# Requesting half of each batch's cache pages from ScalarE's queue in a two-layer hybrid decoder step

## The chip, the cores and the metric

One core of one Trainium2 chip runs the whole program. The metric is the time of one execution in device microseconds (us), median of three runs. Engines are named as in the profile: PE is TensorE, PEld its weight load, DVE VectorE, ACT ScalarE, POOL GpSimd, SP SyncE, which computes nothing and asks for transfers. A q behind a name (SPq, ACTq) is the sequencer of that engine: register work, semaphore waits, DMA issues.

## What is computed

Two decoder layers, for 256 prompt tokens and 8 batches of 8 sample tokens that share all weights. A layer is four parallel token mixers between an input and an output projection, then a feed-forward block. The part that the change touches is the attention of the sample tokens on a paged cache: each of the 8 batches reads its own 8 pages of 128 rows by a page table.

```python
def mla_sample_attention(q_abs, q_pe, ckv, kpe, past):
    ...
    s_past = (jnp.einsum('bqhr,bkr->bhqk', q_abs, pc) + jnp.einsum('bqhp,bkp->bhqk', q_pe, pp)) * scale
    s_new = (jnp.einsum('bqhr,bkr->bhqk', q_abs, ckv) + jnp.einsum('bqhp,bkp->bhqk', q_pe, kpe)) * scale
    ...
    p = jax.nn.softmax(jnp.concatenate([s_past, s_new], axis=-1).astype(jnp.float32), axis=-1)
    return jnp.einsum('bhqk,bkr->bqhr', p[..., :P], pc) + jnp.einsum('bhqk,bkr->bqhr', p[..., P:], ckv)
```

## The kernel before, in words

**Order.** A hardware loop runs the layer body twice. Each engine has a program of its own, written out by hand, and engines meet at semaphores: `ev` counts an event up, `at` gives the value to wait for. Weights stand in HBM as blocks of 128 x 2048 float32 (1 MB) in the order of use, and go through a ring of three buffers, `ring`. SP walks through the blocks in one loop: `load_block(n)` (L950) waits until PE is done with block n-3 and asks for block n. Where the walk reaches certain blocks, SP does other transfers too.

**Splitting.** An input projection block is used in three parts. ACT copies each half of it to a rounded form `wh` (`high`, L1063, two copies of 1024 columns), POOL subtracts it from the block to get the rest, `wlx` (L2015), and PE multiplies with both (L429, L430, then L434). So PE can't start a projection tile before ACT's copy of its half.

**The stretch of the sample batches** is a loop over b = 0 to 7 on each engine. On PE (L820 to L833) iteration b does `sample_back(b-2)`, `sample_turn(b-1)`, `sample_scores(b)` (L736: queries against the 8 pages of batch b, after a wait for all 8), `sample_values(b-1)` (L760), and then a slot of other work that keeps PE busy: gate tiles (the split kind), `branch` blocks (L413) or adaLN blocks, `ada` (L463, with transposes at L453). On ACT (L1323 to L1333) iteration b copies out results of the earlier batches (`sample_back`, `sample_turned`), does the softmax exponentials of batch b (`sample_exp`: one of 128x512 and one of 64x64), in iteration 3 also the squares for the convolution's norm (`conv_squares`), and then what its slot needs: `high` for a coming gate block, sigmoids of gates, copies of ada rows to `rowb`. All of ACT's rows have line 1046, that of the helper `go`.

```python
SLOTS = [[("gate", 2, 0)],
         [("ada", 8), ("gate", 2, 2), ("ada", 9)],
         [("ada", 10), ("ada", 11), ("ada", 12)],
         [("ada", 13), ("ada", 14), ("ada", 15)],
         [("branch", 2, 0), ("gate", 2, 4), ("ada", 16)],
```

**Pages.** The cache has two buffers of 8 pages, one for even and one for odd batches, in `arena`. `load_pages(b)` (L963) runs on SP. It reads the 8 page numbers from SBUF into registers (`value_load`, L965: a TENSOR_LOAD and two register instructions each), waits until PE has done `sample_values(b-2)`, the last reader of that buffer (semaphore pe_m, label so), and issues 8 DMAs (L973) of 128 rows x 2560 B, 320 KB each. For b from 2 on it stands behind the load of block `SLOT_START[b - 1] + 2`, and the loads of the next blocks stand behind it.

Of the kernel before, what the change touches and what calls it, by code (L numbers as in the profile page):

```python
# [24 lines left out]
D_MODEL, SEQ, DEPTH, NB, TS, PAST, PAGE = 1024, 256, 2, 8, 8, 1024, 128  # L25
# [9 lines left out]
NPG = PAST // PAGE  # L35
POOL = NB * NPG * 5 // 4
# [148 lines left out]
class Counts:  # L185
# [21 lines left out]
    def at(self, name, label):  # L207

        return self.sem(name), self.known[name, label] if self.known else 1


def decoder_program(nc, a, known):

    ctx = ExitStack()
    with ctx:
        place = {}

        def sb(name, shape, dt=F32):
            place[name] = (nc.sbuf_base + 31) // 32 * 32
            return ctx.enter_context(nc.sbuf_tensor(name, shape, dt))  # L220
# [5 lines left out]
        C = Counts(nc, ctx, known)  # L226
        ev, at = C.ev, C.at
# [41 lines left out]
        pages = sb("pages", [1, NB * NPG], I32)  # L269
# [5 lines left out]
        def part(n, shape, names, rows=P, start=None):  # L275
            o = used[0] if start is None else start
            v = arena[:, o:o + n].rearrange(f"p ({names}) -> p {names}", **shape) if shape else arena[:, o:o + n]
            if start is None:
                used[0] += n
            assert o + n <= ARENA  # L280
            return v
# [26 lines left out]
        cache = part(2 * NPG * 640, dict(r=2, g=NPG, f=640), "r g f")  # L308
# [73 lines left out]
        with nc.Fori(0, DEPTH) as layer:  # L382
            with nc.Block() as block:
# [556 lines left out]
                def _(sp):  # L940
# [21 lines left out]

                    def load_pages(b):  # L963
                        r = b % 2
                        pgs = [sp.value_load(pages[0:1, b * NPG + g:b * NPG + g + 1], min_val=0, max_val=POOL - 1) for g in range(NPG)]  # L965
                        if b >= 2:
                            sp.wait_ge(*at("pe_m", ("so", b - 2)))
                        else:

                            sp.wait_ge(*at("dve_dc", (NB - 1, 3)))  # L970
                            sp.wait_ge(C.sem("out_state_dp" if b == 0 else "out_state_d"), 16)
                        for g, pg in enumerate(pgs):
                            sp.dma_start(cache[:, r, g, :], a["cache"][lay, bass.ds(pg, 1), :, :].rearrange("l n p f -> (l n p) f")  # L973
                                         ).then_inc(C.sem(f"in_cache{r}"), 16)

                    first_gate = BLOCKS.index(("in", "g0_0", "g0_1"))
                    for n in range(NBLK):
# [37 lines left out]
                        if n == SLOT_START[0]:  # L1015
                            load_pages(0)
# [4 lines left out]
                        if n == SLOT_START[0] + 1:  # L1021
                            load_pages(1)

                        for b in range(2, NB):
                            if n == SLOT_START[b - 1] + RING - 1:
                                load_pages(b)
# [14 lines left out]
                def _(act):  # L1041
                    act.wait_ge(C.sem("in_small"), 16)

                    def go(sem, label, out, in_, func, **kw):
                        in_turn(act, "act")
                        return nc.scalar.activation(out, in_, func, **kw).then_inc(*ev(sem, label))  # L1046
# [5 lines left out]
                    def m(name):  # L1052
                        act.wait_ge(*at("pe_m", name))
                        return banks[name]

                    def ada(a0, a1):
                        for i in range(a0, a1):
                            ps = z(("ada", i))
                            if i >= 2:
                                act.wait_ge(*at("pe_m", ("adaT", i // 2 - 1)))  # L1060
                            go("act_mod", i, rowb[:, i % 2, :], ps[:, 0:256], ACT.Copy)
# [218 lines left out]
                    def conv_squares():  # L1280
                        act.wait_ge(C.sem("out_conv"), 32)
                        for j in range(4):
                            act.wait_ge(*at("dve_c", ("mu", j)))
                            go("act_cy", ("sq", j), sqc[:, j, :], y[:, 2, j, :], ACT.Square)

                    def conv_silu():
                        go("act_cy", "std", std[:], m("conv var")[:, 0:T], ACT.Sqrt, bias=cs("eps")[:, 0:1], scale=1.0 / CCH)
                        for j in range(4):
                            act.wait_ge(*at("dve_c", ("xn", j)))
                            go("act_cy", j, y[:, 2, j, :], y[:, 2, j, :], ACT.Silu, bias=sw("clb", j), scale=sw("clg", j))  # L1290

                    def sample_exp(b):
                        r = b % 2
                        act.wait_ge(*at("dve_s2", ("nm", b)))
                        if b >= 2:
                            act.wait_ge(*at("pe_m", ("sT", b - 2)))
                        go("act_s", ("e", b, 0), pb[:, r, 0:512], m(("ss", b))[:, :], ACT.Exp, bias=stats[:, 100 + r:101 + r], scale=BSCALE,
                           accum_out=stats[:, 104 + 2 * r:105 + 2 * r])
                        go("act_s", ("e", b, 1), pb[0:NS, r, 512:576], pb[0:NS, r, 512:576], ACT.Exp,
                           bias=stats[0:NS, 100 + r:101 + r], scale=BSCALE, accum_out=stats[0:NS, 105 + 2 * r:106 + 2 * r])  # L1300

                    def sample_turned(b):
                        if b >= 2:
                            act.wait_ge(*at("pe_m", ("so", b - 2)))
                        go("act_s", ("pT", b), pT[:, b % 2, 0:512], m(("sT", b))[:, :], ACT.Copy)

                    def sample_back(b):
                        ps = m(("soT", b))
                        go("act_s", ("oT", b), olatT[:, :, :, b * TS:(b + 1) * TS], ps[:, 0:2 * NS].rearrange("p (c h t) -> p c h t", c=2, h=BH), ACT.Copy)

                    def slot(b):
                        for kind, *which in SLOTS[b]:
                            if kind == "gate":
                                gates(*which, count=2, follow=which[0] == 1)
                            elif kind == "branch" and which == [2, 0]:
                                high(SPLIT.index(("in", "g2_4", "g2_5")))
                            elif kind == "ada":
                                nxt = BLOCKS[BLOCKS.index((kind, which[0])) + 1]
                                if nxt in SPLIT and which[0] < 18:
                                    high(SPLIT.index(nxt))  # L1320
                                ada(which[0], which[0] + 1)

                    for b in range(NB):  # L1323
                        if b >= 2:
                            sample_back(b - 2)
                        if b >= 1:
                            sample_turned(b - 1)
                        sample_exp(b)
                        if b == CONV_NORM:
                            conv_squares()  # L1330
                        slot(b)
                        if b == CONV_NORM:
                            conv_silu()  # L1333
# [915 lines left out]
```

## Time and profile before

| | |
|---|---|
| median of 3 runs | 1873.16 us (1868.24 to 1875.08) |
| the profiled execution | 1869.28 us |
| its span, first to last instruction | 1867.3 us |
| PE busy | 1706.9 us, 91% of the span |
| DVE, ACT, POOL busy | 43%, 39%, 38% |
| mean granted PE clock | 0.96 of full |
| DMA | 309 MB, mean 166 GB/s |
| stretch of the sample batches | about 431 to 600 us, and 1359 to 1528 us |

Times of rows are in us from the span's start. Busy rows of a timeline merge neighbouring instructions of one kind; the bracket behind a row gives the idle time of the engine before it and what ended it. The two layers repeat each other closely, so the first stands for both where nothing else is said.

### The profile page before, as it was taken

What the parts mean: (1) busy time and instruction counts of PE and PEld (TensorE: products, weight loads), DVE (VectorE), ACT (ScalarE), POOL (GpSimd) and SP (SyncE); (2) the same over time, 40 slices, a digit from 0 to 9 for tenths busy, and PEclk for the clock granted to TensorE, in tenths of its full rate; (3) what the DMA queues carried; (4) which work ended last, traced back from release to release, by engine and by line L of the source; (5) the groups of instructions that cost most, each with busy time, mean ns of one, the idle gap of its engine ahead of it and who ended that gap; (6) DMA issues with size and microseconds to landing.
All of it is one profiled execution on the core that took longest, in us unless ns stands there. A gap on an engine that the chain in (4) does not pass through costs nothing.

```text
span 1867.3 us, 30317 instructions
## 1 busy us (share of the span) xinstructions
PE 1706.9 (91%) x10994; PEld 1470.4 (79%) x10994; DVE 806.9 (43%) x1887; ACT 735.0 (39%) x1110; POOL 700.8 (38%) x438
## 2 busy tenths in 40 slices
PE   3899999999799989999838999999997999899997
PEld 1788899886477869999717888998864778799996
DVE  0445386655331353332314544876553223533233
ACT  1455534334333244442314564442333432444332
POOL 0434555544122423333113445564531234233331
PEclk9899999999899989999968999999998999899999
DMA  9243335248765344443072523362587643434440
GB/s 352 97 177 114 102 108 204 91 164 305 282 228 201 118 181 149 145 159 135 29 287 91 188 92 102 111 215 85 176 313 281 240 171 127 183 141 157 148 145 29
DMA packets 73246, 309.10 MB, mean 166 GB/s; under 512 B 15554, under 2 KB 25090, under 8 KB 43010
## 3 DMA queue, kind: packets, MB, share of 16 engines
q1 hardware_dynamic: 73090, 307.09, 45.8%
q8 instruction: 90, 1.47, 0.3%
q14 instruction: 66, 0.54, 0.1%
HBM read 291.81 MB, written 15.25 MB: 164 GB/s over the span
## 4 chain that ended last, share of the span: by engine, by line
PE 39%; DVE 6%; DMA 2%; issue 1%; ACT 1%; SPq 1%; DVEq 0%; ACTq 0%
PE zps L429 5%; PE zps L434 5%; PE zps L430 4%; PE zps L890 4%; PE zps L891 4%; PE zps L892 4%; PE zps L413 4%; DMA ring<-wpack_dram 1%; PE mps L736 1%; PE mps L413 1%; DVE arena L1689 1%; PE mps L760 1%; DMA arena<-cache_dram 1%; PE zps L463 1%; PE mps L641 1%
## 5 line engine op out<-in xcount | busy, mean ns | idle before, releaser
L2015 POOL TENSOR_TENSOR wlx<-ring,wh 128x1024 fp32r<-128x1024 f32 x172 | 409.3, 2379 | 708.1 <-ACT wh L1046 702.2
L429 PE MATMUL zps<-uhi,wh 128*128 128x320 f32 x1232 | 380.4, 321 | 1.8 <-ACT wh L1046 1.7
L430 PE MATMUL zps<-ulo,wh 128*128 128x320 f32 x1232 | 367.7, 311 | 0.0
L1046 ACT ACTIVATE wh<-ring 128x1024 fp32r<-128x1024 f32 x172 | 182.3, 1060 | 356.2 <-PE zps L430 252.7
L2115 POOL TENSOR_TENSOR wlo<-ring,whi 128x1024 fp32r<-128x1024 f32 x66 | 160.2, 2427 | 311.2 <-ACT whi L1046 310.3
L429 PEld LDWEIGHTS zps<-uhi,wh 128*128 128x128 f32 x1232 | 235.0, 191 | 14.4 <-issue 9.2
L430 PEld LDWEIGHTS zps<-ulo,wh 128*128 128x128 f32 x1232 | 235.0, 191 | 0.8
L890 PE MATMUL zps<-xhi,whi 128*128 128x320 f32 x688 | 213.8, 311 | 0.0
L891 PE MATMUL zps<-xlo,whi 128*128 128x320 f32 x688 | 213.3, 310 | 0.0
L892 PE MATMUL zps<-xhi,wlo 128*128 128x320 f32 x688 | 213.2, 310 | 0.0
L434 PE MATMUL zps<-uhi,wlx 128*128 128x320 f32 x1248 | 210.5, 311 | 0.0
L434 PEld LDWEIGHTS zps<-uhi,wlx 128*128 128x128 f32 x1248 | 191.1, 190 | 0.1
L1046 ACT ACTIVATE whi<-ring 128x1024 fp32r<-128x1024 f32 x132 | 140.1, 1061 | 102.0 <-PE zps L892 93.9
L413 PE MATMUL zps<-y,ring 128*128 128x320 f32 x512 | 143.9, 438 | 1.0 <-issue 1.0
L1046 ACT ACT_TABLE_LOAD x74 | 94.9, 1283 | 113.0 <-PE mps L736 43.2
L890 PEld LDWEIGHTS zps<-xhi,whi 128*128 128x128 f32 x688 | 130.0, 189 | 0.0
L891 PEld LDWEIGHTS zps<-xlo,whi 128*128 128x128 f32 x688 | 130.0, 189 | 0.0
L892 PEld LDWEIGHTS zps<-xhi,wlo 128*128 128x128 f32 x688 | 129.8, 189 | 0.0
L413 PEld LDWEIGHTS zps<-y,ring 128*128 128x128 f32 x512 | 96.6, 192 | 42.0 <-issue 4.1
L1956 DVE TENSOR_TENSOR wlo<-ring,whi 128x1024 fp32r<-128x1024 f32 x64 | 78.4, 1226 | 102.0 <-ACT whi L1046 101.6
L890 PE MATMUL zps<-hhi,whi 128*128 128x320 f32 x352 | 111.3, 316 | 3.4 <-DVE hlo L1990 3.4
L463 PE MATMUL zps<-ring,siluc 128*32 128x256 f32 x768 | 59.5, 438 | 58.9 <-DMA ring<-wpack_dram 58.9
(279 smaller groups left out, 2548.6 us busy)
## 6 DMA issues: line engine op xcount, KB each, us to landing
ring<-wpack_dram SPq DMA_DIRECT2D x222, 1024.0 KB, 4.9
arena<-cache_dram SPq DMA_DIRECT2D x128, 320.0 KB, 4.9
arena<-stateA_dram SPq DMA_DIRECT2D x2, 2064.0 KB, 9.7
o_cn_s<-arena SPq DMA_DIRECT2D x2, 2064.0 KB, 11.2
arena<-stateD_dram SPq DMA_DIRECT2D x2, 2048.0 KB, 11.9
o_ret_s<-arena SPq DMA_DIRECT2D x2, 2048.0 KB, 11.6
x<-o_y SPq DMA_DIRECT2D x2, 1280.0 KB, 10.1
o_y<-x SPq DMA_DIRECT2D x4, 640.0 KB, 3.0
```

The costliest lines, as they stand in the source:

```text
L413: last = nc.tensor.matmul(o, l, r, start=i == 0, stop=i == len(mms) - 1)
L429: nc.tensor.matmul(o, hi[:, k * P:(k + 1) * P], xh[:, k, :], start=k == 0, stop=False)
L430: last = nc.tensor.matmul(o, hi[:, k * P:(k + 1) * P], xl[:, k, :], start=False, stop=False)
L434: last = nc.tensor.matmul(o, wlx[:, n % RING, (j * KC + k) * P:(j * KC + k + 1) * P], xh[:, k, :], start=False, stop=k == KC - 1)
L463: last = nc.tensor.matmul(ps[g:g + 32, 0:256], siluc[:, k, :], w[:, k * 256:(k + 1) * 256], start=k < 4, stop=k >= 4)
L890: nc.tensor.matmul(o, hi[:, cols], xh, start=start, stop=False)
L891: nc.tensor.matmul(o, hi[:, cols], xl, start=False, stop=False)
L892: return nc.tensor.matmul(o, lo[:, cols], xh, start=False, stop=stop)
L1046: return nc.scalar.activation(out, in_, func, **kw).then_inc(*ev(sem, label))
L1956: V().tensor_tensor(wlo[q % 2][:, 0:1024], ring[:, FFN_AT[q] % RING, 0:1024], whi[q % 2][:, 0:1024], ALU.subtract).then_inc(*ev("dve_w", q))
L2015: G().tensor_tensor(wlx[:, n % RING, half], ring[:, n % RING, half], wh[:, i, :], ALU.subtract).then_inc(*ev("pool_l", (q, i)))
L2115: G().tensor_tensor(wlo[q % 2][:, 1024:2048], ring[:, FFN_AT[q] % RING, 1024:2048], whi[q % 2][:, 1024:2048], ALU.subtract).then_inc(*ev(" ...
```

## The change

SP asks for all 8 pages of batches 0 and 1 as before, but only for pages 0 to 3 of batches 2 to 7. ACT gets a `load_pages` of its own, with its own register loads and its own wait, and asks for pages 4 to 7 of batch b+1 in iteration b (1 to 6), between `sample_exp(b)` and the rest of the iteration. PE's wait for 8 pages is as before.

```diff
                     def load_pages(b):
                         r = b % 2
-                        pgs = [sp.value_load(pages[0:1, b * NPG + g:b * NPG + g + 1], min_val=0, max_val=POOL - 1) for g in range(NPG)]
+                        mine = range(NPG) if b < 2 else range(NPG // 2)
+                        pgs = [sp.value_load(pages[0:1, b * NPG + g:b * NPG + g + 1], min_val=0, max_val=POOL - 1) for g in mine]
...
+                    def load_pages(b):
+
+                        r, half = b % 2, range(NPG // 2, NPG)
+                        pgs = [act.value_load(pages[0:1, b * NPG + g:b * NPG + g + 1], min_val=0, max_val=POOL - 1) for g in half]
+                        act.wait_ge(*at("pe_m", ("so", b - 2)))
+                        for g, pg in zip(half, pgs):
+                            act.dma_start(cache[:, r, g, :], a["cache"][bass.ds(layer, 1), bass.ds(pg, 1), :, :].rearrange("l n p f -> (l n p) f")
+                                          ).then_inc(C.sem(f"in_cache{r}"), 16)
+
                     for b in range(NB):
                         if b >= 2:
                             sample_back(b - 2)
                         if b >= 1:
                             sample_turned(b - 1)
                         sample_exp(b)
+                        if 1 <= b < NB - 1:
+                            load_pages(b + 1)
                         if b == CONV_NORM:
                             conv_squares()
                         slot(b)
```

On ACT, in iteration 1, this stood between the second exponential and the split of gate block g2_2 before:

```order
L1046 ACT_TABLE_LOAD [waits act_s,pe_m]
L1046 ACTIVATE arena,stats<-mps,stats 128x512 [waits dve_s2]
L1046 ACTIVATE arena,stats<-arena,stats 64x64 [waits act_s]
L1046 ACTIVATE wh<-ring 128x1024 [waits pool_l,act_s,pe_h,w_landed0]
L1046 ACTIVATE wh<-ring 128x1024 [waits act_hq,pool_l,pe_h]
L1046 ACTIVATE rowb<-zps 128x256 [waits act_hq,pe_m,pe_z]
```

and this stands there now (line 1047 is 1046 of before; TENSOR_LOAD with two ISA rows is there four times, ISA with DMA four times):

```order
L1047 ACTIVATE arena,stats<-arena,stats 64x64 [waits act_s]
L1327 TENSOR_LOAD pages
L1327 ISA x2
...
L1330 ISA [waits pe_m]
L1330 DMA arena<-cache_dram 128x640
...
L1047 ACTIVATE wh<-ring 128x1024 [waits pool_l,act_s,pe_h,w_landed0]
```

The split copies now come behind four register loads, a wait for PE and four DMA issues of the same queue. The other five iterations, 2 to 6, get the same piece.

## Rows read from the trace of the kernel before

**Rows 1.** The page, part 1: busy us, share of the span, instructions.

```profile
PE 1706.9 (91%) x10994; PEld 1470.4 (79%) x10994; DVE 806.9 (43%) x1887; ACT 735.0 (39%) x1110; POOL 700.8 (38%) x438
```

**Rows 2.** Waits, 400 to 600 us, then 1330 to 1530 us: total, times, longest.

```profile
PE mps L736 <- DMA arena<-cache_dram: 6.7, 3, 5.8
...
PE mps L736 <- DMA arena<-cache_dram: 6.4, 2, 6.2
```

**Rows 3.** Timeline of PE, iterations 1 to 4: start, us, instruction, idle before and releaser.

```profile
450.39 0.39 PE L429 MATMUL zps<-uhi,wh 128*128 128x320 f32 x1 [0.86 <-ACT wh L1046]
...
476.79 3.68 PE L736 MATMUL mps<-arena,qabs 128*64 128x512 f32 x8 [5.84 <-DMA arena<-cache_dram]
...
490.56 0.66 PE L453 MATMUL mps<-const,rowb 128*128 128x128 f32 x4 [1.46 <-ACT rowb L1046]
...
501.27 0.45 PE L413 MATMUL mps<-ckv,qabs 128*64 128x64 f32 x4 [2.21 <-ACT arena L1046]
```

**Rows 4.** Timeline of SP's DMA issues for batches 2 and 3, and blocks behind.

```profile
448.80 4.74 SPq L973 DMA_DIRECT2D arena<-cache_dram  x8
...
466.15 4.80 SPq L973 DMA_DIRECT2D arena<-cache_dram  x8
471.13 1.93 SPq L961 DMA_DIRECT2D ring<-wpack_dram  x3
```

**Rows 5.** Line 965, 442 to 448 us: duration ns, first and last start.

```profile
L965 SPq TENSOR_LOAD <-pages x8: 263/266/272, 442.5 to 446.4; - x8
```

**Rows 6.** Timeline of ACT, iteration 1.

```profile
445.81 1.28 ACT L1046 ACT_TABLE_LOAD   x1 [2.54 <-PE mps L736]
...
448.64 0.35 ACT L1046 ACTIVATE arena<-arena,stats 64x64 f32<-64x64 f32 x1
...
449.19 2.23 ACT L1046 ACTIVATE wh<-ring 128x1024 fp32r<-128x1024 f32 x2
```

**Rows 7.** Line 1070, 448 to 449 us, first sequencer instruction after that exponential.

```profile
L1070 ACTq EVENT_SEMAPHORE  x1: 17/17/17, 448.6 to 448.6; - x1
```

**Rows 8.** Stretches: us, PE, PEld, DVE, ACT, POOL busy, PEclk, DMA share, GB/s.

```profile
466.00:468.00 2.00, 2.00 (x32) 1.09 (x28) 1.23 (x5) 0.83 (x4) 0.00 (x0) 1.00 0.44 119
468.00:470.00 2.00, 2.00 (x35) 1.25 (x24) 0.09 (x2) 0.38 (x1) 0.00 (x0) 1.00 0.85 256
470.00:472.00 2.00, 0.95 (x8) 0.64 (x7) 1.97 (x6) 1.26 (x3) 0.00 (x0) 1.00 0.85 300
472.00:474.00 2.00, 0.00 (x0) 0.00 (x0) 1.08 (x4) 0.00 (x0) 0.00 (x0) 1.00 0.94 321
474.00:476.00 2.00, 0.00 (x0) 0.00 (x0) 0.00 (x0) 0.00 (x0) 0.00 (x0) 0.58 1.05 417
...
480.00:482.00 2.00, 2.00 (x10) 0.55 (x8) 0.04 (x1) 0.00 (x0) 0.00 (x0) 0.72 1.01 422
...
677.00:679.00 2.00, 2.00 (x9) 2.00 (x9) 1.73 (x3) 1.92 (x2) 0.97 (x1) 0.50 0.00 0
```

**Rows 9.** Timeline of PE, first matmul of the feed-forward block.

```profile
672.91 1.41 PE L898 MATMUL zps<-xhi,whi 128*128 128x320 f32 x4 [3.74 <-ACT xhi L1046]
```

**Rows 10.** Timeline of ACT, iteration 3: second exponential, squares.

```profile
485.03 0.35 ACT L1046 ACTIVATE arena<-arena,stats 64x64 f32<-64x64 f32 x1
...
487.86 2.16 ACT L1046 ACTIVATE acc<-y 128x320 f32<-128x320 f32 x4 [2.38 <-DVE y L1834]
```

**Rows 11.** Timeline of ACT, iterations 4, 5 and 6: first work after the exponentials.

```profile
505.12 2.23 ACT L1046 ACTIVATE wh<-ring 128x1024 fp32r<-128x1024 f32 x2
...
535.80 1.28 ACT L1046 ACT_TABLE_LOAD   x1 [3.22 <-PE zps L434]
...
558.64 1.06 ACT L1046 ACTIVATE wh<-ring 128x1024 fp32r<-128x1024 f32 x1 [2.06 <-PE zps L430]
```

**Rows 12.** Timeline of PE: where those gate tiles are used.

```profile
516.02 0.55 PE L429 MATMUL zps<-uhi,wh 128*128 128x320 f32 x1
...
565.43 1.34 PE L434 MATMUL zps<-uhi,wlx 128*128 128x320 f32 x8
```

## The prediction

> **What bounds the kernel now.** I read the page first: PE is busy for 91% of the span [rows 1], so time can be won only in PE's gaps and is lost wherever PE is made to wait. In the waits of the sample stretch the pages cost PE 6.7 us in the first layer and 6.4 us in the second, nearly all of it in one wait per layer [rows 2]: PE sits 5.84 us at the scores of batch 3 [rows 3]. That is what the change could win. The timeline of SP shows the reason: the eight requests for batch 3 go out from 466.15 us, when the buffer has just come free, and take 4.80 us to issue; three ring blocks follow at 471.13 [rows 4]. The timelines of PE and ACT then show what the change could cost: PE already waits for ACT's `wh` copy in iteration 1 (0.86 us), for a `rowb` copy in iteration 3 (1.46 us) and for a copy at the scores of batch 4 (2.21 us) [rows 3]. ACT is on the path exactly there, though it is busy only 39% of the span [rows 1].
>
> **What a batch costs ACT.** Four register loads: on SP eight of them start from 442.5 to 446.4 us, 0.56 us apart [rows 5], so four take 2.2 us. Four issues: SP's eight take 4.74 us [rows 4], 0.59 each, so four take 2.4 us. No row shows ACT doing either; from below I bound the sum at 3.5 us (4 x 0.27 us, the loads without what follows them, and 2.4 us), from above at 6 us (a third more for each instruction), and take SP's 4.6 us, the same instructions on another sequencer. Where do they start? In program order they follow the second exponential. The first sequencer instruction behind it now, a wait for something long done, is at 448.6 us [rows 7], when that exponential starts (448.64) and not when the table load before it went out (445.81) [rows 6]. So ACT's sequencer gets free about at the start of the second exponential, and I count from there.
>
> **Iteration 1 (pages of batch 2).** 448.64 + 4.6 = 453.2 us: the `wh` copies start then instead of at 449.19 [rows 6], 4.05 us later. The wait for PE's values of batch 0 costs nothing, since SP passes the same wait at 448.8 [rows 4]. PE waits for this copy already [rows 3], so nothing covers it: **+4.05 us**, and PE stands still for 4.9 us. After the gap of 3.74 us at 672.91 [rows 9] the granted clock was 0.50 of full, the 1.2 GHz level, still at 677 to 679 [rows 8]; in the 5.84 us gap it fell to a mean of 0.58 in 474 to 476 us, and came back during 480 to 482 (0.72, so low for 1.1 us of it) [rows 8]. There it cost half of the 4.3 us from 476.8 to 481.1, 2.2 us. For iteration 1 I take **+2.5 us**, between nothing (the clock holds) and 3.1 us (half of the 6.1 us from 672.9 to 679).
>
> **Iteration 2 (pages of batch 3).** ACT's copies of ada rows come up to 4 us later, and PE's transposes with them; the cover is PE's wait for pages until 476.79 [rows 3]. The question is when the last page lands. SP's half is out by 468.6 us, as before. ACT's half starts at 466.1 + 2.2 = 468.3 and is out by 470.7, no sooner than pages 4 to 7 were. The pages are not limited by the issuing alone: while they move, the DMA engines are 85 to 94% busy at 256 to 321 GB/s [rows 8]. Had they been the limit of nothing, 2.3 us of issuing saved would come back whole; as it is, the best case is 1 us sooner. New is that SP's three ring blocks (3 MB) are now asked for at 468.7, 2.4 us sooner, on one queue, beside ACT's pages on another. By 469.5 us SP's half has moved about 0.6 MB of its 1.31 MB (2 us at 119 and 1.5 us at 256 GB/s [rows 8]). At equal shares of 300 GB/s its rest ends near 474.1, ACT's half having moved 0.7 MB too; the last 0.6 MB of ACT's run beside the ring blocks. If both queues get equal bytes of 420 GB/s [rows 8], they land at 477.1, 0.3 us later than now; if they take turns row by row, 2560 B against 8192 B, ACT's get a quarter, 100 GB/s, and land at 480.3, 3.5 us later. I take the middle, **+2.0 us**, with -1 and +3.5 as ends. The Trainium skill ("DMA: Bandwidth & Descriptors", section on queues, rings and completion order) says that an engine takes turns between queues packet by packet; by that rule alone the sum would stand at the upper end, and no row of before shows two data queues at once. The same page (issuing engines are not separate DMA queues) holds that issuing from several engines saves only issue time; the busy shares of 85 to 94% agree.
>
> **Iteration 3 (pages of batch 4).** From 485.03, ACT is held until 489.65; the squares start at 487.86 now [rows 10], so they come 1.8 us later. Behind them is the `rowb` copy for which PE waits at 490.56 [rows 3], then the variance, the convolution's norm and the copy for which PE waits at 501.27: **+1.8 us**. This also covers pages of batch 4 that land up to about 4 us late.
>
> **Iterations 4 to 6: nothing.** In 4 the copies at 505.12 [rows 11] slide by 4 us as in iteration 1, to about 509.3, and are used from 516.02 [rows 12]; PE's branch block is the cover. In 5 the table load at 535.80 came after 3.22 us of idle time, so the second exponential started 3.66 us ahead of it, and it slides by 0.9 us. In 6 the copy at 558.64 [rows 11], with 2.06 us of idle time ahead, slides by 2.1 us; its half is multiplied from about 563 and its rest at 565.43 [rows 12], after POOL's 2.4 us, which leaves some 1 us. If PE's cover were gone each would cost what it slides. SP's shorter issue brings ring blocks sooner, but PE waits for none of them there.
>
> **Sum.** 4.05 + 2.5 + 2.0 + 1.8 = 10.35 us per layer, 20.7 us for two. The profiled execution took 1869.3 us, so 1890.0; it lay 3.9 us under the median, so against the median of 1873.2 I forecast **1893.9 us**, 1.1% slower. From the ends: least 2 x (2.95 + 0 - 1 + 0.7) = 5.3 us, if ACT's loads and issues take 3.5 us; most 2 x (5.45 + 3.1 + 3.5 + 3.2) = 30.5 us.
>
> **Rivals.**
> - *ACT's sequencer runs ahead.* The Trainium skill ("Perfetto Trace Analysis", section on DVE and ACT instructions) says that a sequencer is free once it has pushed an instruction into a wait queue. As a mechanism of this kernel: the loads run in the time in which ACT waits for DVE's maximum, from 445.8 on, and only the issues (2.4 us from 448.6) are left. Iteration 1 then costs 451.0 - 449.2 = 1.8 us, iteration 3 nothing (its issues end at 487.5, before the squares), and batch 3's pages, all asked for by 468.5, land 1 us sooner: 2 x 0.8 = 1.6 us, 1875. For it: ACT idles 2.54 us ahead of that table load [rows 6]. Against it: rows 7. Chance 0.12.
> - *The clock holds and the pages aren't late.* Only ACT's stalls are left: 2 x 5.85 = 11.7 us, 1885. For it: PE had stood still for 3 us by 474, at a clock still at 1.00 [rows 8]. Part of the forecast's family; 0.2.
> - *The pages of batch 3 come early enough, the other side.* If two queues moved them 3.8 us sooner (landing by 473), PE's gap there would be 2 us, the 2.2 us of low clock would go too, and with the run-ahead of the first rival the layer would win 3.8 + 2.2 - 1.8 = 4.2 us: 1865. It decides only where the landing comes forward by more than ACT's own delay on the path, 1.8 us at the least and 5.85 us by my count. Against it: the 2.6 MB of a batch need 6.2 us even at 420 GB/s, from 467.4 at the earliest, so 473.6 at best. Chance 0.04.
> - *The change doesn't do what it says.* The order of instructions shows 4 of 8 requests on ACT for six batches; only batches 0 and 1 are left out. Chance nil.
>
> **How the numbers follow.** Forecast as summed 0.64, only the stalls 0.2, run-ahead 0.12, faster 0.04. About 0.5% (9.4 us) is what a measurement of this kernel can tell from no change. The two first cases are over it but for their lower edge, 0.06 of them: slower 0.78; same 0.06 + 0.12 + part of the last = 0.19; faster 0.03. The range runs from 1881 (stalls at the short end) to 1904 (all costs at their upper ends); it leaves out the run-ahead, the faster case and the tails.
>
> **What would show it.** Right: 48 of 128 page requests on ACT's sequencer, some 4.6 us from the first register load to the last issue; PE's wait on `wh` at the first split tile of iteration 1 near 5 us with a stretch of clock 0.50 behind it; PE's wait on `rowb` in iteration 3 over 3 us; the wait for pages of batch 3 no shorter than before. Wrong: register loads on ACT ahead of the exponentials, a page wait well under 4 us, or an unchanged wait in iteration 1.

## The result and the profile after

The changed kernel takes 1905.73 us (median of 4 runs, 1903.99 to 1906.86); the kernel before, with one more run beside it, 1870.76 us. The ratio is 1.0189, with a 95% interval of 1.0169 to 1.0209. Forecast were 1893.9 us and a range of 1881 to 1904: the sign was right, the size was not. The sum gave 20.7 us; about 35 us were lost.

The change does what it says. From the DMA table of the changed kernel (engine, count, KB each, median us from issue to landing):

```profile
arena<-cache_dram SPq DMA_DIRECT2D x80, 320.0 KB, 4.3
arena<-cache_dram ACTq DMA_DIRECT2D x48, 320.0 KB, 7.2
```

48 of 128 page requests are ACT's, and they land later after their issue than SP's do. PE's timeline in the first layer, against [rows 3]:

```profile
455.13 0.60 PE L429 MATMUL zps<-uhi,wh 128*128 128x320 f32 x1 [5.27 <-ACT wh L1047]
...
479.04 0.66 PE L453 MATMUL mps<-const,rowb 128*128 128x128 f32 x4 [2.52 <-ACT rowb L1047]
...
490.68 3.68 PE L736 MATMUL mps<-arena,qabs 128*64 128x512 f32 x8 [9.97 <-DMA arena<-cache_dram]
...
506.80 1.12 PE L453 MATMUL mps<-const,rowb 128*128 128x128 f32 x4 [3.91 <-ACT rowb L1047]
...
515.69 1.94 PE L736 MATMUL mps<-arena,qabs 128*64 128x512 f32 x8 [1.50 <-DMA arena<-cache_dram]
```

The wait for `wh` grew from 0.86 to 5.27 us, that for pages of batch 3 from 5.84 to 9.97, with 2.52 us for `rowb` ahead of it, and in iteration 3 there are 3.91 us for `rowb` and 1.50 for pages of batch 4. In the second layer the same waits are 5.29, 10.38, 3.66 and, for batch 4:

```profile
1461.73 3.68 PE L736 MATMUL mps<-arena,qabs 128*64 128x512 f32 x8 [4.33 <-DMA arena<-cache_dram]
```

The times between the first score matmuls (L736) of consecutive batches, from the timelines of both kernels, show where the 37.6 us between the two profiled spans (1867.3 and 1904.9) lie. The rest of the program adds 0.4 us.

| us, first layer / second | before | after |
|---|---|---|
| batch 1 to 2 (iteration 1) | 17.4 / 17.4 | 24.2 / 24.3 |
| batch 2 to 3 | 16.9 / 17.4 | 23.6 / 24.3 |
| batch 3 to 4 | 19.3 / 18.5 | 25.0 / 25.0 |
| batch 4 to 5 | 29.9 / 30.4 | 27.5 / 30.4 |
| batches 5 to 7 | 45.2 / 45.2 | 45.2 / 45.2 |

ACT's timeline in iteration 1 and SP's and ACT's issues for batch 3, against [rows 4, 6]:

```profile
448.96 0.35 ACT L1047 ACTIVATE arena<-arena,stats 64x64 f32<-64x64 f32 x1
449.22 0.19 ACT L1047 ACTIVATION_READ_ACCUMULATOR arena<-arena,stats 64x1 f32 x1
451.57 2.18 ACTq L1330 DMA_DIRECT2D arena<-cache_dram  x4
453.93 2.23 ACT L1047 ACTIVATE wh<-ring 128x1024 fp32r<-128x1024 f32 x2 [4.53 <-issue]
...
475.56 2.42 ACTq L1330 DMA_DIRECT2D arena<-cache_dram  x4
```

```profile
473.31 2.06 SPq L974 DMA_DIRECT2D arena<-cache_dram  x4
475.57 1.53 SPq L961 DMA_DIRECT2D ring<-wpack_dram  x3
```

ACT's queue needs 4.97 us from the second exponential to the copies (forecast 4.6). For batch 3, ACT's first request goes out in the same hundredth of a microsecond as SP's first ring block. The stretches around it (columns as in [rows 8]):

```profile
474.00:476.00 2.00, 2.00 (x36) 1.32 (x36) 0.66 (x3) 0.00 (x0) 0.00 (x0) 1.00 0.79 265
476.00:478.00 2.00, 0.52 (x12) 0.04 (x4) 0.00 (x0) 0.00 (x0) 0.00 (x0) 1.00 0.95 291
478.00:480.00 2.00, 0.96 (x9) 0.96 (x10) 0.27 (x1) 0.99 (x3) 0.00 (x0) 1.00 1.07 396
...
486.00:488.00 2.00, 0.00 (x0) 0.00 (x0) 0.00 (x0) 0.00 (x0) 0.00 (x0) 0.50 1.01 423
488.00:490.00 2.00, 0.00 (x0) 0.00 (x0) 0.00 (x0) 0.00 (x0) 0.00 (x0) 0.50 0.68 271
```

By 478 us the engines have moved 1.1 MB, all of it from SP's half of the pages (1.3 MB). In the DMA records of this trace (one for each row moved) ACT's first row starts at 478.12 us and the first ring row at 478.06. All of ACT's half then goes beside 3 MB of ring blocks, at 396 to 423 GB/s in total, and both end together near 490.

### The profile page after: what moved, and what is told of

Its sections match the earlier page's. It is cut to its first block and busy times, and to the rows that moved or that the text cites. A ratio compares the mean times of both kernels' runs of the same rounds, so it can differ in the third digit from the quotient of the medians.

```text
span 1904.9 us, 30321 instructions
## 1 busy us (share of the span) xinstructions
PE 1713.8 (90%) x10994; PEld 1476.3 (78%) x10994; DVE 799.8 (42%) x1887; ACT 735.0 (39%) x1110; POOL 700.5 (37%) x438
## 5 line engine op out<-in xcount | busy, mean ns | idle before, releaser
L429 PE MATMUL zps<-uhi,wh 128*128 128x320 f32 x1232 | 383.5, 323 | 10.7 <-ACT wh L1047 10.6
L1047 ACT ACTIVATE whi<-ring 128x1024 fp32r<-128x1024 f32 x132 | 140.1, 1061 | 101.4 <-PE zps L892 93.9
## 6 DMA issues: line engine op xcount, KB each, us to landing
o_cn_s<-arena SPq DMA_DIRECT2D x2, 2064.0 KB, 11.4
arena<-stateD_dram SPq DMA_DIRECT2D x2, 2048.0 KB, 11.9
```

The lines of the kernel that those rows point to most:

```text
L429: nc.tensor.matmul(o, hi[:, k * P:(k + 1) * P], xh[:, k, :], start=k == 0, stop=False)
```

## The experiments

**1. Nothing on ACT in iteration 1.**

```diff
-mine = range(NPG) if b < 2 else range(NPG // 2)      # SP
+mine = range(NPG) if b < 3 else range(NPG // 2)
-if 1 <= b < NB - 1: load_pages(b + 1)                # ACT
+if 2 <= b < NB - 1: load_pages(b + 1)
```

> Edit: SP asks for all eight pages of batch 2; ACT asks for its half only for batches 3 to 7, so iteration 1 has no page work on ACT. Theory (ACT's stall in front of the wh copies, with the low clock behind it, is a term of its own): PE's wait at the first split tile of iteration 1 falls from 5.3 us back to 0.9, no clock of 0.5 follows at 454 us, the scores of batch 2 start near 460 us as before the change; 2 x (4.4 + 2.4) = 13.6 us come back, about 1892 us. The wait for pages of batch 3 stays at 10 us. Rival (all of the loss is that pages land late): iteration 1 costs nothing net, the time stays within 3 us of 1905.7.

Measured: 1891.87 us, ratio to before 1.0115 (1.0082 to 1.0149). PE's timeline:

```profile
450.27 0.38 PE L429 MATMUL zps<-uhi,wh 128*128 128x320 f32 x1 [0.85 <-ACT wh L1047]
...
483.93 3.68 PE L736 MATMUL mps<-arena,qabs 128*64 128x512 f32 x8 [10.34 <-DMA arena<-cache_dram]
```

Batch 1 to 2 takes 17.4 us again in both layers, so ACT's stall and the low clock behind it cost 6.8 and 6.9 us there, and 13.9 us of the median went, as forecast. The pages of batch 3 stay as late: a term of its own.

**2. Ring blocks held back until the pages have landed.**

```diff
 if n == SLOT_START[b - 1] + RING - 1:
     load_pages(b)
+    sp.wait_ge(C.sem(f"in_cache{b % 2}"), 16 * NPG * (b // 2 + 1))
```

> Edit: the changed kernel, but SP waits until all eight pages of a batch (2 to 7) have landed before it asks for the next ring blocks, so no ring row shares the DMA engines with ACT's pages. Theory (ring blocks on SP's queue take three quarters of the bandwidth from ACT's pages): pages of batch 3 land 7 us or less after ACT's last request, PE's wait for them falls from 10 us to between 4 and 7 us, the extra wait for pages of batch 4 goes; 4 to 8 us come back, about 1899 us, less what PE then waits for late ring blocks. Rival (ACT's pages are late because ACT asks late, or because its queue is slow): the landing from ACT's queue stays near 12 us in iteration 2 and the time rises, as ring blocks come later too.

Measured: 1889.65 us, ratio 1.0106 (1.0068 to 1.0144), more than forecast. Line 1331, ACT's requests for batch 3, and PE's timeline:

```profile
DMA to landing us min/median/max: 4.9/5.2/5.8
```

```profile
488.23 3.68 PE L736 MATMUL mps<-arena,qabs 128*64 128x512 f32 x8 [2.47 <-DMA arena<-cache_dram]
```

In the changed kernel the same requests took this long:

```profile
DMA to landing us min/median/max: 7.9/11.7/13.3
```

With no ring block beside it ACT's queue is about as quick as SP's was before the change (median 5.2 us against 4.9), and PE's page wait falls to 2.5 us, with 2.13 us for `rowb` ahead of it. So the ring blocks were what made the pages late. Batch 2 to 3 takes 16.0 us in both layers, 0.9 and 1.4 us less than before the change: PE starts the scores of batch 3 9.7 us after SP's first request, where the kernel before needed 10.6 and 11.1, although ACT still asks 2.2 us after SP. That is a small gain of two queues. Late ring blocks cost PE nothing that its waits show in the stretch. In the first layer batch 0 to 1 took 16.0 us instead of 11.4, at a clock of 0.50 from 434 to 444 us; but SP asks for batch 2 only at 455.43 us, and the edit first acts behind that, so this isn't its doing.

**3. The register loads alone, in the kernel before.**

```diff
 sample_exp(b)
+if 1 <= b < NB - 1:
+    for g in range(NPG // 2, NPG):
+        act.value_load(pages[0:1, (b + 1) * NPG + g:(b + 1) * NPG + g + 1], min_val=0, max_val=POOL - 1)
```

> Edit: the kernel before, with ACT's four register loads in iterations 1 to 6 and nothing else of the change. It prices the loads: 4 x 0.56 = 2.2 us behind the second exponential. Theory (ACT's sequencer doesn't run ahead): the wh copies of iteration 1 start 1.8 to 2.2 us later, PE waits 2.7 to 3.1 us there; iteration 3 costs nothing (487.3 is before 487.86); 2 x 2 = 4 us slower, up to 8 if the clock falls after a gap of 3 us: 1875 to 1879. Rival (the sequencer runs ahead and the loads are free): same as before within 1 us.

Measured: 1875.44 us, ratio 1.0024 (1.0002 to 1.0046). PE waits 2.82 us for `wh` in the first layer, 2.60 in the second. ACT's timeline:

```profile
447.78 0.35 ACT L1046 ACTIVATE arena<-arena,stats 64x64 f32<-64x64 f32 x1
448.04 0.19 ACT L1046 ACTIVATION_READ_ACCUMULATOR arena<-arena,stats 64x1 f32 x1
450.30 2.23 ACT L1046 ACTIVATE wh<-ring 128x1024 fp32r<-128x1024 f32 x2 [2.08 <-issue]
```

2.08 us of ACT's idle time follow the exponential: the loads don't run ahead of it, and four of them cost about what SP's rows said (2.2 us). Scores of batch 0 to those of batch 7 take 142.7 and 142.3 us, against 140.1 and 140.2.

**4. The register loads ahead of the exponentials, in the changed kernel.**

```diff
+if 1 <= b < NB - 1:
+    pgs = page_numbers(b + 1)      # the four value_loads
 sample_exp(b)
 if 1 <= b < NB - 1:
-    load_pages(b + 1)
+    load_pages(b + 1, pgs)         # the wait and the four requests
```

> Edit: the changed kernel, with ACT's four register loads ahead of the exponentials, where ACT waits for DVE's maximum, and its wait and four requests where they were. Theory: the loads are covered in part (ACT idles 2.3 us ahead of the table load and 1.0 behind it), so the stall behind the exponentials shrinks from 4.5 to about 2.3 us: PE's wait in iteration 1 falls from 5.3 to about 3.1, that for rowb in iteration 3 by 2, and ACT asks 2.2 us sooner in iteration 2, so that ACT's pages get onto the engines ahead of the ring blocks and land 3 us sooner. 2 x 5 to 2 x 8 us come back: 1890 to 1896. Rival (the late pages don't depend on when ACT asks): 2 x 3 us come back, 1900.

Measured: 1877.42 us, ratio 1.0032 (1.0013 to 1.0052), far more than either expected: 28.3 of 35 us came back. The issues for batch 3, SP's and ACT's, and what PE waits:

```profile
468.39 2.05 SPq L974 DMA_DIRECT2D arena<-cache_dram  x4
470.62 1.50 SPq L961 DMA_DIRECT2D ring<-wpack_dram  x3
```

```profile
L1334 ACTq DMA_DIRECT2D arena<-cache_dram x4: 348/356/375, 468.5 to 470.2; - x4
...
DMA to landing us min/median/max: 3.8/5.9/9.0
```

```profile
479.27 3.42 PE L736 MATMUL mps<-arena,qabs 128*64 128x512 f32 x8 [5.99 <-DMA arena<-cache_dram]
```

With the loads out of the way ACT asks at 468.5 us beside SP's 468.39, its last request 0.4 us ahead of the first ring block, and the pages are there 10.9 us after SP's first request, where one queue alone needed 10.6 [rows 3, 4]. In the changed kernel it was 17.4 us, so 2.2 us in the time of asking decide over 6.5 us in the landing. The DMA records tell why: from 472 to 476 us the two queues moved 291 and 314 rows of pages, and the first ring row comes at 475.92, when about nine tenths of the page rows have started. In this order of requests two queues win nothing: the wait for batch 3 is 5.99 us, where it was 5.84. It is not the best that the change could do. ACT's last rows still run beside ring blocks here, and with the ring blocks held back (experiment 2) the pages came about 1 us sooner than from one queue. Both edits together were not run.

**5. and 6. Narrower ring rows.**

```diff
-sp.dma_start(ring[:, n % RING, :], src).then_inc(C.sem(f"w_landed{n % RING}"), 16)
+for h in range(2):
+    sp.dma_start(ring[:, n % RING, h * 1024:(h + 1) * 1024], src[:, h * 1024:(h + 1) * 1024]).then_inc(C.sem(f"w_landed{n % RING}"), 16)
```

(waits for `w_landed` count by 32 then)

> Edit: the changed kernel, each ring block asked for as two DMAs of 4096 B rows instead of one of 8192 B; nothing else. Theory (while both queues have work, the DMA engines take one row from each in turn): beside 4096 B rows ACT's 2560 B rows get 38% instead of 24% of the bandwidth, so the 512 rows of ACT's half pass at about 60 per us instead of 39 and pages of batch 3 land 3 to 4 us sooner; PE's wait falls from 10 us to 6 or 7 us and the one at batch 4 goes; 6 to 10 us come back over the two layers, about 1897 us, less what the doubled ring requests cost (see the control). Rival (equal bytes for each queue, or the later request alone): the wait stays at 10 us within 1 us.

> Edit: the kernel before with the same split ring blocks, as the control of the run above. Both theories: one queue alone, so no change in sharing; the second request costs SP 0.5 us a block, hidden behind PE. Within 3 us of before.

Measured: 1909.52 us, ratio 1.0190 (1.0148 to 1.0232); the control 1876.39, ratio 1.0030 (1.0003 to 1.0057). The waits for pages of batch 3 in the two layers:

```profile
491.50 3.68 PE L736 MATMUL mps<-arena,qabs 128*64 128x512 f32 x8 [6.67 <-DMA arena<-cache_dram]
...
1443.34 3.68 PE L736 MATMUL mps<-arena,qabs 128*64 128x512 f32 x8 [8.71 <-DMA arena<-cache_dram]
```

They fell by 3.3 and 1.7 us and the wait for batch 4 went. Part of the 3.3 us only moved to `rowb` (3.20 us instead of 2.52); from SP's first request to the scores it is 1.6 and 1.9 us less, where 3 to 4 were forecast. The time did not fall. From the scores of batch 0 to those of batch 7 the kernel takes 156.1 and 154.4 us (changed kernel 156.9 and 160.5), but outside of that the profiled execution loses 11.8 us. The control's loses 1.8 there, so the doubled requests alone don't explain it; why stays open. What settles how two queues share is the DMA records, rows started by each queue:

| | ring rows (SP's queue) | page rows (ACT's queue) |
|---|---|---|
| changed kernel, 480 to 488 us, ring rows of 8192 B | 310 | 304 |
| experiment 5, 484 to 489 us, ring rows of 4096 B | 304 | 300 |

In the second layer they are 307 and 324, and 302 and 301. The counts are near equal however wide the ring's rows are: turns by row, not by bytes. ACT's pages went from 38 to 60 rows per us, as the theory said, and with equal bytes they would have had some three rows for each ring row in the first case.

**7. Keys before values, one queue.** The scores read only a page's key part, the values only the rest, so the key part's space is free a good part of an iteration earlier. The edit is to the kernel before; PE then waits for each part where it reads it, and the host packs a page's keys ahead of its values.

```diff
-sp.wait_ge(*at("pe_m", ("so", b - 2)))
+sp.wait_ge(*at("pe_m", ("ss", b - 2)))
-    sp.dma_start(cache[:, r, g, :], a["cache"][lay, bass.ds(pg, 1), :, :]...).then_inc(C.sem(f"in_cache{r}"), 16)
+for part_, c0, c1 in (("keys", 0, 3 * P), ("values", 3 * P, 5 * P)):
+    if part_ == "values" and b >= 2:
+        sp.wait_ge(*at("pe_m", ("so", b - 2)))
+    for g, pg in enumerate(pgs):
+        sp.dma_start(cache[:, r, g, c0:c1], a["cache"][lay, bass.ds(pg, 1), :, c0:c1]...).then_inc(C.sem(f"in_{part_}{r}"), 16)
```

> Edit: the kernel before, all requests on SP, but a page comes as two DMAs: its key part (1536 B rows, read by the scores) is asked for when the scores of batch b-2 are done, its value part (1024 B rows, read by the values) when the values of batch b-2 are done; the host packs the page's columns as keys, rotary keys, values. Theory (the 5.8 us wait for pages of batch 3 is there because all of a page is asked for only when the last reader of its buffer is done): the key parts of batch 3 go out from about 464 us instead of 466.15 and in half the bytes, and land near 472 us, when PE gets there at 471; the wait falls to 0 to 2 us, the low clock behind it goes; 2 x 5 to 2 x 7.5 us: 1855 to 1860. Rival (the stretch is bound by what the DMA engines move, 5.8 MB between 466 and 484 us): PE waits for the ring blocks of ada 13 instead, and the time stays within 5 us of before.

Measured: 1868.67 us, ratio 0.9989 (0.9968 to 1.0009): no change, and neither theory as told. PE's timeline:

```profile
455.14 0.39 PE L429 MATMUL zps<-uhi,wh 128*128 128x320 f32 x1 [3.09 <-ACT wh L1050]
...
478.44 1.94 PE L736 MATMUL mps<-arena,qabs 128*64 128x512 f32 x8 [1.28 <-DMA arena<-cache_dram]
...
489.66 1.07 PE L463 MATMUL zps<-ring,siluc 128*32 128x256 f32 x16 [1.44 <-DMA ring<-wpack_dram]
```

The wait for batch 3 did fall to 1.3 us in the first layer, where the matmuls run at full clock (1.94 us instead of 3.68), and to 1.7 in the second, where they stay slow (3.50). It was lost again in iteration 1: SP's 16 requests for batch 1 take 8.9 us and stand ahead of the ring block of which `wh` is made.

**8. Experiments 1 and 4 together.** Both edits, in the changed kernel.

> Edit: the changed kernel with the register loads ahead of the exponentials and ACT's half only from batch 3 on, so nothing is left in front of the wh copies of iteration 1. Theory: PE's wait there falls from 2.8 to 0.9 us; 2 x 1.9 = 3.8 us less than 1877.4, about 1873; what is left of the change is a wash, since the wait for pages of batch 3 stays near 6 us (two queues move the pages no faster than one). Rival (two queues do help once ACT asks early): the wait for pages of batch 3 below 5 us and the time under 1868.

Measured: 1875.39 us (about 1873 expected), ratio 1.0009 (0.9982 to 1.0035), no difference from before that can be told. Page waits at batch 3 of 5.90 and 7.12 us: with the ring blocks right behind them, two queues move the pages no faster than one.

**9. Keys before values, whole pages for batches 0 and 1.** Against experiment 7:

```diff
-for part_, c0, c1 in (("keys", 0, 3 * P), ("values", 3 * P, 5 * P)):
+for part_, c0, c1 in (("keys", 0, 3 * P), ("values", 3 * P, 5 * P)) if b >= 2 else (("keys", 0, 5 * P),):
```

> Edit: the version with key parts before value parts, but batches 0 and 1, whose buffers are free at once, are asked for in whole pages again (8 requests instead of 16). Theory (what that version won at batch 3 it gave back in iteration 1, where 16 requests of SP's for batch 1 pushed the ring block of gate g2_2 back, and where 16 for batch 2 stand ahead of the next blocks): PE's wait for wh in iteration 1 falls from 3.1 and 2.0 us to 0.9, 2 x 2 to 2 x 3.5 us come back, 1862 to 1865. Rival (the loss of iteration 1 has another cause, such as the shorter rows): no change against that version, 1868.

Measured: **1858.47 us**, ratio 0.9947 (0.9929 to 0.9965), better than forecast (1862 to 1865). `wh` is on time again and the page wait stays short:

```profile
450.11 0.39 PE L429 MATMUL zps<-uhi,wh 128*128 128x320 f32 x1 [0.86 <-ACT wh L1051]
...
473.16 2.37 PE L736 MATMUL mps<-arena,qabs 128*64 128x512 f32 x8 [2.46 <-DMA arena<-cache_dram]
```

**10. The same, value parts one ring block later.**

```diff
+if n == SLOT_START[b - 1] + RING:
+    page_parts(b, "values", 3 * P, 5 * P)      # waits for ("so", b - 2), then 8 requests
 if n == SLOT_START[b - 1] + RING - 1:
-    load_pages(b)                              # both parts
+    load_pages(b)                              # key parts
```

> Edit: as the run above, and the value parts of batches 2 to 7 are asked for one ring block later, behind the first of the blocks that follow the key parts. Theory (SP's issue queue is what delays the ring blocks of the ada slots, and the value parts aren't needed for a whole iteration): PE's waits for ring blocks at the ada blocks of iteration 3 go too (1.4 and 0.9 us), batch 3's keys land as soon as before; 1857 to 1863. Rival (bytes bound the stretch, 5.8 MB in 18 us): the same bytes come in another order, and the time stays within 3 us of the run above.

Measured: 1858.92 us, ratio 0.9932 (0.9914 to 0.9950): the same as experiment 9 within noise, which the rival forecast; that bytes are the bound is not shown by it. The waits for ring blocks did not go: PE waits 1.12 and 0.68 us for them in the second layer. Both versions beat the kernel before and the changed one.

## Why the prediction was right and wrong

**ACT's price and place: right.** The loads don't run ahead (experiment 3), the whole piece holds the copies up by 4.4 us where 4.05 were forecast, and with the clock iteration 1 cost 6.8 and 6.9 us against 6.55; experiment 1 gave it back. The four signs named for being right all came, but they test the mechanism of the stall and not the size of the whole. The clock row of the changed kernel behind that wait:

```profile
456.00:458.00 2.00, 2.00 (x10) 2.00 (x9) 0.00 (x0) 0.55 (x2) 1.86 (x2) 0.50 0.98 391
```

**Iteration 2: the mis-sized term.** The forecast was +2.0 us with an upper end of 3.5; 6.7 and 6.9 us were measured. The step that failed is "its rest ends near 474.1, ACT's half having moved 0.7 MB too": I let ACT's bytes flow about one microsecond after its first request and share the engines with SP's pages. In fact 452 of SP's 512 rows had started before ACT's first, and ACT had moved 0.15 MB and not 0.7 when SP's half was through; for ACT asks 2.2 us later than SP and its first row comes 2.6 us behind that, so all 1.3 MB of ACT's went beside the ring blocks, not 0.6 MB. Of the two ways of sharing that I set as ends, turns by row was the right one, by the row counts under experiment 5: 1.31 MB at a quarter of 420 GB/s is 12.5 us, and ACT's rows took 11.9 us from the first to the last. The rule of the Trainium skill ("DMA: Bandwidth & Descriptors", section on queues, rings and completion order) is packet by packet in turn. The equal counts of rows agree with it if the packets of both queues hold as many rows, which no record here shows. The middle between the ends was no estimate but a refusal to choose; the upper end would still have been 3.2 and 3.4 us short, since it left only 0.6 MB for the ring blocks to hold up.

The time from SP's first request for batch 3 to PE's first score matmul puts the runs side by side:

| us, first layer / second | |
|---|---|
| kernel before: one queue | 10.6 / 11.1 |
| changed: ACT asks 2.2 us late | 17.4 / 18.0 |
| experiment 5: the same, ring rows of 4096 B | 15.8 / 16.1 |
| experiment 2: late, but ring blocks held back | 9.7 / 9.7 |
| experiment 4: ACT asks at once | 10.9 / 10.7 |

**Iteration 3: too low.** +1.8 us forecast, 5.7 and 6.5 measured. ACT's stall for `rowb` was +2.4 and +2.2 us, near the forecast. The rest is the sentence that the stall "also covers pages of batch 4 that land up to about 4 us late": they share the engines with ring blocks just as batch 3's do, and PE waited 1.5 and 4.3 us for them, where it had waited 0.5 and 0. In the second layer the two waits make up the whole 6.5 us. In the first they make 3.4 of 5.7; the matmuls from 506.80 to 513 us took 2.4 us more than before, at a clock of 0.50 to 0.53 up to 512, which is the rest. There 2.4 us came back between batches 4 and 5, where the kernel before had its own low stretch.

**Iterations 4 to 6: right**, 45.2 us in both kernels from batch 5 to 7, and no loss from batch 4 to 5. **The rivals.** Run-ahead fell with experiment 3. The faster case, which needed pages 3.8 us sooner, didn't come even when both queues asked at once (experiments 4 and 8), nor with the ring blocks held back, where the gain was about 1 us; the two together are untested. "DMA: Bandwidth & Descriptors" of the Trainium skill says in its section on issuing engines that a second engine saves only issue time, and the 10.9 against 10.6 us agree.

The terms don't add up quite: experiments 1 and 2 give back 14 and 16 us of 35 and experiment 4 alone 28, since an earlier request mends the stall in part and the lateness wholly. In experiment 4 nearly all of what is left lies in iteration 1, 3.4 and 3.5 us.

## What to carry to other kernels

In this kernel a second DMA queue added next to no bandwidth; it added a competitor. If one half of what somebody waits for goes to another queue and arrives there later than the first queue's next large transfers, it is served in turns with them, here row for row, so that narrow rows lose against wide ones, and the whole is as late as its last part. Put instructions on an engine that seems idle only after reading what stands behind them, register loads included, and place them where that engine waits anyway. And where a transfer waits for its buffer, ask first which part of the buffer the next reader needs: that, not the queue, was where the time lay here.

## What the runs showed of the hardware that I had not expected

Moving four register loads, 2.2 us of sequencer time, changed the kernel by 28 us. Two DMA queues with work shared the engines row for row: 304 rows of 2560 B beside 310 of 8192 B in 8 us, and 300 beside 304 of 4096 B in 5 us. So the queue with narrow rows got 97 GB/s in the first case and 154 in the second, and its requests landed up to 13.3 us after issue where 5.8 us was the longest without ring blocks.
